# Stick-breaking layer, first three groups: three attention steps per turn of the job list instead of one

## The reference

```python
def _sb_core(q, k, v, qpos, kpos):
    z = jnp.einsum('bqhd,bkhd->bhqk', q, k).astype(jnp.float32) * (SB_HD ** -0.5)
    valid = kpos[None, :] < qpos[:, None]
    log_beta = jax.nn.log_sigmoid(z)
    log_rem = jnp.where(valid, jax.nn.log_sigmoid(-z), 0.0)
    later = lax.cumsum(log_rem, axis=3, reverse=True) - log_rem
    a = jnp.where(valid, jnp.exp(log_beta + later), 0.0).astype(v.dtype)
    return jnp.einsum('bhqk,bkhd->bqhd', a, v)

def _odd_layer(x, pos, caches, prm):
    w_in, w_out, ln_g, ln_b = prm
    b, s, _ = x.shape
    q, k, v, g = _split_cols(x @ w_in, (SB_W, SB_W, SB_W, SB_W))
    ...
    y = _layernorm(ALPHA * x + o, ln_g, ln_b)
    return y, (k, v)
```

## Time and profile before

| | |
|---|---|
| time, median of 3 runs | 835.0 us (834.83 to 835.03) |
| the profiled execution | 834.43 us, its span 832.6 us |
| PE busy | 804.4 us, 97% of the span |
| DVE busy | 531.0 us, 64% |
| ACT busy | 409.0 us, 49% |
| POOL busy | 74.8 us, 9% |
| TensorE clock granted, in tenths | 9 in every slice of 40 |
| first three groups of layer 1 | 463.5 to 716.5 us of the span |

### The profile page before, as it was taken

One profiled execution on the slowest core, in us unless ns is written; L12 is line 12 of the kernel. 1 busy time (PEld: TensorE's weight loads), 2 busy tenths in 40 slices (PEclk: granted clock), 3 DMA queues, 4 the chain that ended last, 5 costly groups with the idle time before them and its releaser, 6 DMA issues.

```text
span 832.6 us, 16906 instructions
## 1 busy us (share of the span) xinstructions
PE 804.4 (97%) x6588; PEld 701.8 (84%) x6588; DVE 531.0 (64%) x1055; ACT 409.0 (49%) x935; POOL 74.8 (9%) x102
## 2 busy tenths in 40 slices
PE   7999999999999999999999999999999999999994
PEld 5987788888889898778999988888888888887673
DVE  5566366556575657676922656676566776778877
ACT  4234533334444546442334656665567565687710
POOL 2120001000000000001210010001100100121002
PEclk9999999999999999999999999999999999999998
DMA  7731121211423343423232433334323343344203
GB/s 239 177 98 52 51 64 52 71 46 31 139 68 124 100 129 122 144 67 111 88 126 93 130 100 119 101 101 132 115 93 103 123 135 116 104 130 130 67 25 127
DMA packets 67533, 86.25 MB, mean 104 GB/s; under 512 B 6016, under 2 KB 53920, under 8 KB 67456
## 3 DMA queue, kind: packets, MB, share of 16 engines
q1 hardware_dynamic: 63712, 74.47, 29.0%
q0 software_dynamic: 3744, 10.70, 4.0%
HBM read 74.25 MB, written 10.90 MB: 102 GB/s over the span
## 4 chain that ended last, share of the span: by engine, by line
PE 80%; issue 9%; DVE 5%; ACT 3%; POOL 2%; DMA 1%; DVEq 0%; SPq 0%; POOLq 0%; ACTq 0%
PE turn L956 24%; PE pair L956 17%; PE proj L956 15%; PE value L956 15%; PE turn L1005 3%; PE turn L1181 2%; PE value L1005 1%; POOL rstd L929 1%; PE proj L1005 1%; DVE w_words L1615 1%; ACT w_words L1381 1%; PE proj L1181 1%; DVE probs L1734 1%; PE pair L1005 0%; DMA stage<-in_w_in_even_dram 0%
## 5 line engine op out<-in xcount | busy, mean ns | idle before, releaser
L1615 DVE TENSOR_TENSOR w_words<-stage,w_words 128x512 fp32r<-128x512 f32 (+1 forms) x136 | 91.8, 682 | 93.6 <-ACT w_words L1381 93.0
L956 PE MATMUL turn<-w_words,xT_hi 128*128 128x256 f32 (+2 forms) x680 | 144.4, 309 | 1.0 <-DVE xT_lo L1620 0.7
L956 PEld LDWEIGHTS turn<-w_words,xT_hi 128*128 128x128 f32 x680 | 109.3, 191 | 6.2 <-DVE x_sb L1866 1.5
L956 PE MATMUL turn<-w_words,xT_lo 128*128 128x256 f32 (+2 forms) x348 | 104.3, 300 | 0.0
L1381 ACT CAST w_words<-stage 128x512 fp32r<-128x512 f32 (+1 forms) x144 | 87.3, 616 | 28.9 <-DMA stage<-in_w_in_even_dram 14.7
L956 PE MATMUL proj<-w_words,xT_hi 128*128 128x256 f32 (+2 forms) x380 | 76.6, 300 | 0.3
L956 PE MATMUL value<-w_words,xT_hi 128*128 128x256 f32 (+2 forms) x348 | 75.1, 311 | 0.8 <-DVE w_words L1615 0.8
L956 PE MATMUL turn<-xT_hi,w_words 128*128 128x320 f32 x320 | 74.9, 314 | 0.0
L956 PE MATMUL pair<-w_words,xT_hi 128*128 128x512 f32 (+2 forms) x272 | 71.6, 350 | 0.1
L956 PEld LDWEIGHTS turn<-w_words,xT_lo 128*128 128x128 f32 x348 | 66.3, 191 | 2.5
L1457 ACT ACTIVATE work<-pair,peak 128x512 f32<-128x512 f32 (+4 forms) x80 | 40.9, 516 | 45.5 <-DVE peak L1723 45.4
(11 more groups left out here) (519 smaller groups left out, 1715.4 us busy)
## 6 DMA issues: line engine op xcount, KB each, us to landing
stage<-in_w_in_odd_dram SPq DMA_DIRECT2D x64, 256.0 KB, 2.7
stage<-in_w_in_even_dram SPq DMA_DIRECT2D x44, 256.0 KB, 2.8
k_c<-in_cache_sb_k_dram SPq DMA_DIRECT2D x32, 256.0 KB, 3.6
v_c<-in_cache_sb_v_dram SPq DMA_DIRECT2D x32, 256.0 KB, 3.0
mlaK<-in_cache_diff_k_dram SPq DMA_DIRECT2D x8, 512.0 KB, 3.9
mlaK<-in_cache_diff_v_dram SPq DMA_DIRECT2D x8, 512.0 KB, 4.3
stage<-in_w_out_even_dram SPq DMA_DIRECT2D x16, 256.0 KB, 2.6
stage<-in_w_out_odd_dram SPq DMA_DIRECT2D x16, 256.0 KB, 2.7
```

Of the source, the lines that this page charges most:

```text
L956: return nc.tensor.matmul(o, l, r, start=first, stop=last)
L1615: v.tensor_tensor(piece(w_lo[:, sec % 2, words]), piece(stage[:, n % STAGES, :]), piece(w_hi[:, sec % 2, words].bitcast(F32)), ALU.subtrac ...
```

## The change

The first three groups are written by a new function, `stick_triples`. Twelve turns (four a group) take three steps each: two prompt steps `one` and `two` and the `sample` step that follows. In a turn the rows of both scores (the q-k products, now a job `rows` of their own) stand ahead of both masks; the values of the three steps of the turn before stand together behind the turn's third bundle, ahead of and behind the sample's score; `split` says by `PARTS` how many bundles stand in each of five places. Twelve `ROOM` entries are still shared by the same costs, and their bundles joined by threes: 5, 5, 4 and 5 bundles in the turns of the first two groups, 4, 3, 4 and 4 in those of the third, the last of each group holding g or q projections. The samples' turned weights get a buffer of their own, `wT1s`, in free columns of `probs`, and the prompt's two buffers are counted by prompt steps alone. The fourth group keeps `stick_pipeline`, which takes over the last three steps (`before`). No instruction is added or left out.

```diff
@@ -120,7 +120,35 @@
-def stick_pipeline(steps, fills, after, tails):
+PARTS = {3: (1, 1, 0, 0, 1), 4: (1, 1, 1, 0, 1), 5: (1, 1, 1, 1, 1), 6: (1, 1, 2, 1, 1)}
+
+
+def split(bundles):
+
+    out, bundles = [], list(bundles)
+    for n in PARTS[len(bundles)]:
+        out.append(flat_jobs(bundles[:n]))
+        bundles = bundles[n:]
+    return out
+
+
+def stick_triples(steps, fills, after):
+
+    jobs, before = [], []
+    for k in range(0, len(steps), 3):
+        one, two, sample = steps[k:k + 3]
+        part = split(fills[k // 3])
+        jobs += [("rows", one), ("rows", two), ("score", one), ("score", two)] + part[0]
+        jobs += [("turn", before[2])] if before else []
+        jobs += [("cacheT",) + sample + (h,) for h in range(2)] + [("stick", one)] + part[1] + [("weigh", one), ("stick", two)] + part[2]
+        jobs += [("value", s) for s in before[:2]] + [("score", sample)] + [("value", s) for s in before[2:]]
+        jobs += [("turn", one), ("turn2", one), ("weigh", two), ("stick", sample)] + part[3] + [job for s in before for _, job in after(s)]
+        jobs += [("turn", two), ("turn2", two), ("weigh", sample)] + part[4]
+        before = [one, two, sample]
+    return jobs
+
+
+def stick_pipeline(before, steps, fills, after, tails):
...
@@ -130,8 +158,13 @@
     for i, now in enumerate(steps):
         fill = fills[i]
         jobs.append(("score", now))
+        if i == 1:
+            jobs.append(("value", before[2]))
+            later.setdefault(2, []).extend(job for _, job in after(before[2]))
         for bundle in fill[:1]:
             jobs += bundle
+        if i == 0:
+            jobs.append(("turn", before[2]))
         if i >= 2:
             s = steps[i - 2]
             jobs.append(("turn", s))
...
@@ -143,6 +176,8 @@
             if i == max([j - 2, 0] + [k for k in samples if k < j]):
                 jobs += [("cacheT",) + steps[j] + (k,) for k in range(2)]
         jobs += later.pop(i, []) + tails.get(i, [])
+        if i == 0:
+            jobs += [("value", s) for s in before[:2]]
         if i >= 3:
             s = steps[i - 3]
             jobs.append(("value", s))
...
@@ -314,23 +357,28 @@
     for g in range(GROUPS - 1):
         order = [(3, 0), (0, 0), (2, 0), (1, 0), (3, 1), (0, 1), (2, 1), (1, 1)]
         steps += mingle([("B", g, t, blk) for t, blk in order], [("BS", g, p) for p in range(STREAMS // 2)])
-        fills += share(project(g + 1), [ROOM[s] for s in ("3", "0", "S", "2", "1", "S", "3", "0", "S", "2", "1", "S")])
-
+        fills += [flat_bundles(turns) for turns in by_threes(share(project(g + 1), [ROOM[s] for s in "30S21S30S21S"]))]
+
+
+    def after(s):
+        if s[0] == "BS":
+            return [(1, ("bsT", s[1], s[2]))]
+        return [(1, ("otile", s[2]))] if s[1] == GROUPS - 1 and s[3] == 1 else []
+
+    jobs += stick_triples(steps, fills, after)
+    before = steps[-3:]
 
     g = GROUPS - 1
     order = [(3, 0), 0, (2, 0), 1, (3, 1), 2, (2, 1), 3, (1, 0), (1, 1), (0, 0), (0, 1)]
-    steps += [("BS", g, s) if s in range(STREAMS // 2) else ("B", g) + s for s in order]
+    steps = [("BS", g, s) if s in range(STREAMS // 2) else ("B", g) + s for s in order]
     operand, second, right, upper = (convert(name) for name in ("out100", "out110", "out101", "out111"))
 
     six = {t: [("out", 1, 0, t, 0)] for t in tiles}
-    fills += [[[("g", g, 0, 0)] + operand[:2]], [[("g", g, 0, 1)] + operand[2:3], [("sig", g, 0), ("sigm", g, 0)]],
+    fills = [[[("g", g, 0, 0)] + operand[:2]], [[("g", g, 0, 1)] + operand[2:3], [("sig", g, 0), ("sigm", g, 0)]],
               [[("g", g, 1, 0)] + operand[3:], [("silu", g, 0), ("ocvt", 0)]], [[("g", g, 1, 1)], [("silum", g, 0), ("ocvt", 1)] + second[:2]],
               [six[0], [("ocvt", 3)]], [[("sig", g, 1)], [("sigm", g, 1)] + six[1] + [("ocvt", 2), ("silu", g, 1)] + second[2:] + [("silum", g, 1)]],
               [six[3], [("ocvt", S_TILE)]], [six[2]], [], [six[S_TILE]], [[("out", 1, 1, 3, 0)]], []]
-    jobs += stick_pipeline(
-        steps, fills,
-        lambda s: [(1, ("bsT", s[1], s[2]))] if s[0] == "BS"
-        else [(1, ("otile", s[2]))] if s[1] == GROUPS - 1 and s[3] == 1 else [], {len(steps) - 2: right[:2]})
+    jobs += stick_pipeline(before, steps, fills, after, {len(steps) - 2: right[:2]})
 
 
     light, before, first, last = steps[-4:]
...
@@ -532,6 +580,7 @@
         wT1 = flat(work8).rearrange("p (s a n) -> p s a n", s=2, a=2)
         probs0 = wT1
         gtmp = flat(probs)[:, 0:TOK]
+        wT1s = flat(probs)[:, 640:1024]
         newv1 = flat(probs)[:, 1024:1536].rearrange("p (a n) -> p a n", a=2)
 
         def q_blocks(g):
...
@@ -603,7 +652,9 @@
 
         def turned(s, i):
 
-            return wT1[:, nth[s] % 2, i, :] if s in stick_no else wT0[nth[s] % 2][i]
+            if s[0] == "BS":
+                return wT1s
+            return wT1[:, pair_no[s] % 2, i, :] if s in stick_no else wT0[nth[s] % 2][i]
 
         def stick_view(s):
 
...
@@ -1005,6 +1057,17 @@
                     i = nc.tensor.transpose(ps(job)[0:c, c0:c0 + r], src, ident[0:r, 0:r])
                 i.then_inc(filled[where[job][0]], 1)
 
+            def stick_scores(s):
+
+                _, g, t, blk = s
+                for j in range(t + 1):
+                    wait_drained(pe, ("kT", g, j))
+                for part in range(2):
+                    wait_drained(pe, ("q", g, blk, part))
+                for h in range(2):
+                    r = slice(HD * h, HD * h + HD)
+                    mm(ps(("score", s))[:, h, 0:width(s)], qT1[r, g % 2, blk, tok(t)], kT[r, g % 2, blk, 0:width(s)], True, False)
+
             pe.wait_ge(consts_in, 16)
             for job in schedule:
                 kind = job[0]
...
@@ -1083,11 +1146,15 @@
                     pe.wait_ge(kc_in[b % 2], 16 * (4 * g + b // 2 + 1))
                     transposes(job, [((2 * i + half) * P, k_c[:, b % 2, half, i * P:(i + 1) * P])
                                      for i in range(2) for half in range(2)])
+                elif kind == "rows":
+                    wait_bank(pe, ("score", job[1]))
+                    stick_scores(job[1])
                 elif kind == "score":
                     s = job[1]
                     n = width(s)
-                    wait_bank(pe, job)
                     o = ps(job)
+                    if ("rows", s) not in schedule:
+                        wait_bank(pe, job)
                     if s[0] == "M":
                         _, t, pair = s
                         pe.wait_ge(kr_done, PT_TILES)
...
@@ -1138,14 +1205,8 @@
                             m = mm(o[r, PAST:n], qblk[:, b, h, :], dkT[:, h, new(b)], True, True)
                         m.then_inc(done, 1)
                     elif s[0] == "B":
-                        _, g, t, blk = s
-                        for j in range(t + 1):
-                            wait_drained(pe, ("kT", g, j))
-                        for part in range(2):
-                            wait_drained(pe, ("q", g, blk, part))
-                        for h in range(2):
-                            r = slice(HD * h, HD * h + HD)
-                            mm(o[:, h, 0:n], qT1[r, g % 2, blk, tok(t)], kT[r, g % 2, blk, 0:n], True, False)
+                        if ("rows", s) not in schedule:
+                            stick_scores(s)
                         for h in range(2):
                             m = mm(o[:, h, n - P:n], identb[:, :], mask_causal[:, :], False, True)
                         m.then_inc(done, 1)
```

More of the change, by code:

```diff
@@ L184, in beside, with flat_bundles, by_threes @@
     return [b + conversions[len(conversions) * i // n:len(conversions) * (i + 1) // n] for i, b in enumerate(bundles)]
+def flat_bundles(turns):
+    return [bundle for turn in turns for bundle in turn]
+def by_threes(turns):
+    return [turns[i:i + 3] for i in range(0, len(turns), 3)]
 def flat_jobs(bundles):
@@ L674, in trunk_kernel @@
         stick_no = {s: i + 1 for i, s in enumerate(sb_steps)}
+        pair_no = {s: i for i, s in enumerate(s for s in sb_steps if s[0] == "B")}
         last_lower = [j for j in schedule if j[0] == "out" and j[1] == 0 and j[4] == 1 and ("begin", 0, j[3]) not in where][-1]
@@ L1236, in _ @@
                                 m = mm(o[HD * h:HD * h + HD, 0:P], v_n[:, g % 2, j, c0:c0 + HD],
-                                       wT1[:, nth[s] % 2, h, tok(j)], j == 0, j == last)
+                                       turned(s, h)[:, tok(j)], j == 0, j == last)
                     else:
@@ L1487, in _ @@
                     s = job[1]
-                    w = wT1[:, nth[s] % 2, 0, :]
+                    w = turned(s, 0)
                     wait_filled(act, job)
@@ L1497, in _ @@
                     wait_filled(act, job)
-                    nc.scalar.copy(wT1[:, nth[s] % 2, 1, 0:width(s)], ps(job)[:, 0:width(s)]).then_inc(done, 1)
+                    nc.scalar.copy(turned(s, 1)[:, 0:width(s)], ps(job)[:, 0:width(s)]).then_inc(done, 1)
```

## The result

The changed kernel takes 843.45 us (median of 4 runs, 842.8 to 845.1) against 835.0 before: a ratio of 1.0108, 95% interval 1.0093 to 1.0122. That is 8.4 us slower; forecast were 842.0 and 7.0.

A forecast was written before the change was run, and what follows sets the result against it. PE was taken to bound the kernel, busy 249.7 of 253.0 us in the three groups. Shape changes -4.8, waits that go -6.1 and waits that come +17.9 gave +7.0, so 835.0 would become 842.0 us, range 833.5 to 848.

The forecast's parts named there:

- Waits that come, 17.9: New PE waits behind back-to-back score operations on ACT and sticks on DVE, turns 2 to 12 and last group: 17.9 us.
- the copy's end at 6.65: Turn 10: ACT's copy of the first projection bundle, behind six score operations, ends 6.65 us into the turn.
- the gate product's end at 15.8: Turn 10: DVE's chain through the first value's gate product, whose bank turn2 of one takes, ends at 15.8 us.
- that of a wait at turn2 with the longest near 3.5, in turns 9 to 11: Expected trace sign: PE's transpose turn2 waits for DVE's oT product, longest near 3.5 us, in turns 9 to 11.
- Waits that go, 6.1: PE's waits around DVE's copy of a turned prompt step (L1759) all go: 6.1 us saved.
- Shape changes, 4.8: PE saves 0.4 us in each of 12 turns on array shape changes, a value entry and a mask: 4.8 us.
- the rows leave for the mask: On PE, going from a score's rows to its mask was taken to have no visible price.
- The prediction's sum by this rule, 5.3: If every tiling change drains the engine, all 59 vanished changes would pay 0.09: 5.3 us saved instead of 4.8.
- the 0.045 and the 0.08 a turn: PE savings per turn beside the shape changes: one entry into a value, 0.045, and one mask before a projection product, 0.08.
- The last group, 1.0: A new wait of 1.0 us at the last group's first sample score, whose cache half stands behind two splits.
- the faster one: Rival, chance 0.17: DVE reaches the gate product in time; with only first-bundle bank waits of 5 left, 829 us.
- The clock: Rival, chance 0.04: PE's clock falls to 1.2 GHz behind waits of turns 9 to 11, 8.8 us more, 851.

The follow-up runs named there:

- e4: e3 with the rows of two moved directly ahead of their own mask, behind the first bundle: 840.7 us against 839.2.
- f5: e2 with the value of the first prompt step moved ahead of stick two, behind the second bundle, in all 12 turns: 837.2 us.
- e2: The changed kernel with the first bundle, and so ACT's copy of it, moved ahead of score two: 833.9 us, ratio 0.9983.
- h1: e2 with the last bundle moved ahead of turn of two in the six turns with three or four bundles: 829.7 us, ratio 0.9937.
- e1: The changed kernel with stick two moved behind the two prompt values: 848.2 us, ratio 1.0154.
- e3: The changed kernel with both the edit of e1 and that of e2: 839.2 us, ratio 1.0046.
- f6: e2 with, in turns of three or four bundles, value one ahead of stick two and a bundle taken from ahead of the values: 842.6 us.

## Why the prediction was right

- **The time, 842.0 (833.5 to 848), and its sign:** right, 843.45. The sum's terms were less exact than their sum.
- **Waits that come, 17.9:** right in size: 19.3 and 1.9 in the last group, turn by turn within 0.2 but for turn 5 (0.6 more) and turns 1, 2 and 6, where small ones of 0.2 to 0.4 ahead of a projection had no term. The mechanism was right too: in-order engines, with the copy, the cast and the gate product behind two sets of score operations and two sticks. The places were right in part: of the 19.3 about 2.7 are waits for ACT's weigh, in turns 3, 7, 9, 11 and 12, which the prediction names nowhere; for turns 9, 11 and 12 it gives totals without their working, so that these agree says little. ACT's start at 1.87 was 1.66, the copy's end at 6.65 was 6.3, the gate product's end at 15.8 was 15.5. Within turn 10 one wait was missed: the sample's score takes stick one's bank. The prediction had 1.0 at the copy and then the rest at turn2; it is four waits, of 1.0, 1.1, 1.6 and 0.4. So of its signs, that of a wait at turn2 with the longest near 3.5, in turns 9 to 11, did not come: the longest is 1.4, in turn 10, and turn 9 has none. That the four still add up to 4.1 is no accident: the wait at turn2 ends when DVE's chain does, however many shorter ones come ahead of it.
- **Waits that go, 6.1:** right, 5.8 by the same count of starts, and the copy's successor, L1820, is waited for once.
- **Shape changes, 4.8:** this step failed in size. Denser instructions gave 7.9. Two kinds of change stood in the sum at nothing. The first is that the rows leave for the mask: the 0.43 of two passes of 128 columns has this price inside it. By e4 it is 0.1, and another 0.1 goes to the first pass of a block of rows: the rows of two scores take 1.28 us together and 0.85 + 0.64 apart, so 0.20 a turn where 0.09 was in the sum. The second is that the sample's score and the sample's values, both 128*32, now stand together. Before, a score of a sample, the projection products behind it and a sample's values further on:

```profile
521.79 0.64 PE L956 MATMUL pair<-k_cT,qblk 128*32 128x256 f32 x8
...
522.42 0.41 PE L956 MATMUL turn<-xT_hi,w_words 128*128 128x320 f32 x1
522.67 0.31 PE L956 MATMUL turn<-xT_lo,w_words 128*128 128x320 f32 x1
...
527.00 0.65 PE L956 MATMUL proj<-v_c,work 128*32 128x128 f32 x16
```

After:

```profile
521.59 0.64 PE L1008 MATMUL pair<-k_cT,qblk 128*32 128x256 f32 x8
...
522.13 0.62 PE L1008 MATMUL turn<-v_c,probs 128*32 128x128 f32 x16
```

The score takes 0.54 from its start to what follows instead of 0.63, no projection product stands behind it at 0.25 instead of 0.15, and the values cost no change of their own (0.09) and 0.02 less; 0.15 comes back, since the rows no longer follow these values directly and a transpose behind them takes 0.06 more. That makes 0.16 a turn. The values of the prompt together give 0.24, where 0.23 was in the sum, and the masks together 0.07, where 0.08 was. 0.20 + 0.16 + 0.24 + 0.07 = 0.67 a turn, 8.0 in twelve, against the 7.9. (e4's 0.29 and f5's 0.33 are prices of other places, a block behind transposes and a value between bundles.)
- **The rule on changes:** The Trainium skill, "TensorEngine Tiling (Array Packing)", Key Properties, states that every change of the tiling mode drains the engine. The trace agrees: each change that was read here costs 0.09 to 0.1 us, that from rows to mask among them. The prediction's sum by this rule, 5.3, is short as well, because it left out the 0.045 and the 0.08 a turn that its own sum has beside the changes; with them it is 59 x 0.093 + 12 x 0.125 = 7.0.
- **The last group, 1.0:** 2.2, at the fourth score, which had no term, and 0.5 at the cache transposes.
- **The rivals:** the faster one did not come, but e2 shows how near it was: ACT lets the copy through sooner, by the place of one job, and the kernel is faster than before. It is 833.9 and not 829, since 9.9 us of waits stay and not 5; that h1 comes to 829.7 is chance, because it moves the last bundle too. The clock did not fall between 13 and 836 us in the profiled execution of the changed kernel; it fell in e1, e3, e4 and f6. (In both kernels it is at 0.50 in the last 5 to 6 us of the span, so the last of the 40 slices before shows 8 and not 9.)

The misses cancel in part, and that much of the closeness is luck: 3.1 more saved than forecast, against 0.3 less in waits that go, 2.4 more in waits of the three groups, 1.2 in the last group and 0.6 at the start: 7.0 became 8.4.

## What to carry to other kernels

When two steps of an in-order pipeline are joined, list on each engine what now stands behind both, and ask who frees a bank there: a copy of 0.4 us and the cast behind it, held up by six operations, cost 9.5 us in twelve turns, and moving them ahead of one job turned a loss of 1% into a gain of 0.2%. Joining products of one shape is worth it (0.7 us a turn here) once the cover stays: put independent work between a result and its use, and take none from ahead of a bank that is emptied late. Price a shape change from two jobs that differ in their neighbour alone, never from a step that may already hold the price.

## What the runs showed that I had not expected

Where PE goes 1.7 us or more from one start to the next, the clock falls to its lower level in some executions and not in others of the same program. Four traces have such falls, seven in all, each 3.4 us at 0.50: e1 three, e4 two, e3 and f6 one each. Each begins inside such a step or at most 1.3 us behind its end. In e1 one is worth 1.55 us, with 845.7 to 850.7 us between its runs. The length of the step doesn't decide it: the changed kernel has steps of 1.7 and 2.0 us, e2 of 1.7 and 1.8, and their profiled executions have no fall. What does decide it stays open. And the start of the stage moves by 2.3 us between traces (462.7 to 465.0) before anything that the kernels have different.
